# The first projection stage with on-chip transfers in place of the permutation matmul of the rotary embedding

## The chip, the cores and the metric

The kernel runs on one core of a Trainium2 chip. The metric is the device time of one execution in microseconds. Shown beside it is one execution taken by the hardware profiler. The engines are TensorE (PE; PEld is its weight load), VectorE (DVE), ScalarE (ACT), GpSimd (POOL) and SyncE (SP), which here only issues DMAs.

## The reference

The model has two blocks of the first kind (an attention mixer, then a gated linear attention mixer) and one block with pooling, convolution, forgetting attention and a mixture of experts. Only the first mixer's projection concerns us. For 1024 tokens and 256 context tokens it computes `h @ w_in` (1024 features in, 26 x 128 out), normalizes the q and k heads (64 features each), and rotates the q and k of the tokens, not those of the context:

```
def rope_1d(x, pos):
    m = x.shape[-1] // 2
    inv = ROPE_BASE ** (-jnp.arange(m, dtype=jnp.float32) / m)
    ang = pos.astype(jnp.float32)[:, None] * inv[None, :]
    cos = jnp.cos(ang)[:, None, :]
    sin = jnp.sin(ang)[:, None, :]
    x1 = x[..., :m].astype(jnp.float32)
    x2 = x[..., m:].astype(jnp.float32)
    return jnp.concatenate([x1 * cos - x2 * sin, x2 * cos + x1 * sin], axis=-1)
...
def rope_axial(x, rows, cols):
    h = x.shape[-1] // 2
    return jnp.concatenate([rope_1d(x[..., :h], rows), rope_1d(x[..., h:], cols)], axis=-1).astype(x.dtype)
...
def project(h):
    ...
    qa = rms_norm(qa.reshape(Bn, T, A_HEADS, HEAD_DIM), a_qn)
```

The halves of a rotated pair are 16 features each, so in blocks of 32 features the first 16 and the last 16 change places, with a minus sign on one of them.

## The kernel before

Features lie on the 128 partitions and tokens along the free axis. `gemm_phase` (line 375) runs a list of jobs. A 32-bit matmul such as `rot` or `headones` shows in the trace as two records. A job makes 128 output features for all 1280 tokens: 8 contraction steps, in each of them three products (high x high, high x low, low x high parts of 32-bit numbers), each over three tiles of 512, 512 and 256 tokens, into one of two PSUM accumulators. In the first projection stage there are 26 jobs. Jobs 0 and 2 to 13 are q or k ("rope"); job 1 and jobs 14 to 25 are stored as they are ("store"). Jobs 0 and 1 run interleaved.

The engines run their own programs and meet at semaphores:

- SP loads the weight tiles into a ring of three (line 527); tile w waits until the low half of tile w-3 has been made (w_lo).
- ScalarE rounds the weights (line 583) and, when a rope job's products are done, writes for each tile its square into `sq` (line 715) and the accumulator times the gain into `xg` (line 716). The latter gives `free`, the accumulator's release (acc_free in the order).
- TensorE computes the helper matmuls of a rope job inside the products of the next job: one tile after every second contraction step (line 1104, `rope_aux`). For a tile of tokens these are `rot` times `xg` (line 1077, the permutation) and `headones` times `sq` (line 1079, the sums of squares of each head). For the context tile only the second is made. Before the helper matmuls of tile r TensorE waits for `rope_done` of the tile before it.
- ScalarE makes the reciprocal root from the sums (lines 609 and 611). VectorE multiplies the permuted piece by the sine table (line 1001) and `xg` by the cosine table (line 1002), adds them (line 1003) and multiplies by the root in place (line 1006), which gives `rope_done`. Then the piece is split into high and low halves and stored.
- Later phases issue other transfers from SP that the rows below show: `wa` (two loads of 17 partitions x 512), `rank` (two of 16 partitions x 1280), `k_lo` and `q_stack` (64 partitions x 1280, twelve loads in a row), `q_rows` and `gate` (64 partitions x 2 x 128).
- VectorE and GpSimd also compute the conditioning vectors of the second block in this stage (line 569 loads, line 807 products). Three preparing steps of these stand behind jobs 2, 3 and 4 on VectorE; the second of them is a reciprocal over 2048 columns (line 794).

Of the kernel before, what the change touches and what calls it, by code (L numbers as in the profile page):

```python
# [19 lines left out]
ALU = mybir.AluOpType  # L20
# [3 lines left out]
P = 128  # L24
D = 1024
KD = D // P
T = 1024
CTX = 256
META = 16
L2 = META + T  # L30
X0 = META
# [37 lines left out]
def shape_constants():  # L69

    p = np.arange(P)
    parts = {}
# [3 lines left out]

    rot = np.zeros((P, P))
    for d in range(P):
        if d % 32 < 16:
            rot[d + 16, d] = -1.0  # L80
        else:
            rot[d - 16, d] = 1.0
    parts["rot"] = rot
    m = 16
# [3 lines left out]
    ang = np.zeros((P, T), np.float32)  # L88
    for d in range(P):
        pos = rows if d % HD < 32 else cols  # L90
        ang[d] = pos.astype(np.float32) * inv[d % 16]
    parts["cos"], parts["sin"] = np.cos(ang), np.sin(ang)

# [32 lines left out]

CONST_WIDTHS = [("ident", P), ("ones", P), ("headones", P), ("rot", P), ("causal", P), ("anti", P), ("invcnt", 2 * META)]
ROUTE_WIDTHS = [("before", P), ("tile_end", 7), ("tile_at", 16), ("spare_off", 16), ("tile_no", 15), ("bound", NTILE + 1), ("column", P),
# [246 lines left out]
def gemm_phase(nc, E, wts, jobs, feed, adaln=None, decay_rows=None, spill=None, restore=None, sums=False, branch=None):  # L375
# [7 lines left out]
    with ExitStack() as ctx:  # L383
# [54 lines left out]
        if "rope" in kinds:  # L438
            xg = sb("rope_x", [P, 1280])
            sq = sb("rope_sq", [P, 1280])  # L440
            tab = sb("rope_tab", [P, 2, T])
            t1 = sb("rope_t1", [P, 512])
            t2 = sb("rope_t2", [P, 512])
            rs = sb("rope_rs", [P, 512])
            slots = [t1[:], t2[:], sq[:, 0:512], sq[:, 512:1024]]
            aux = [ps("rope_ss", [P, 512]), ps("rope_rot", [P, 512])]
            tab_in, xg_ready, aux_done, rope_done, ms_ready, rs_ready = (
                sem(n) for n in ("tab_loaded", "xg_ready", "aux_done", "rope_done", "mean_square_ready", "rstd_ready"))
# [66 lines left out]
        def _(eng):  # L515
            def load_operand(i):
# [3 lines left out]
                eng.dma_start(staged(i), feed.src(k, off, n)).then_inc(fed_in[i % feed.ring], 16)  # L520

            if feed.src is not None:
                load_operand(0)
            for w in range(wts.loaded, NW):
                if w >= NSTG:
                    eng.wait_ge(w_lo, w - NSTG + 1)
# [8 lines left out]
                if w == 8 and spill is not None:  # L535
                    eng.dma_start(spill, E.X[:, :, 0:META + T]).then_inc(spilled, 16)
            if spill is not None:
                eng.wait_ge(spilled, 16)
# [218 lines left out]
        def _(eng):  # L757
# [220 lines left out]
            for i, j in enumerate(jobs):  # L978
# [7 lines left out]
                for t, (off, n) in enumerate(j.tiles):  # L986
# [9 lines left out]
                    elif j.kind == "rope":  # L996
# [3 lines left out]
                        if off < T:  # L1000
                            eng.tensor_tensor(t2[:, 0:n], aux[1][:, 0:n], tab[:, 1, off:off + n], ALU.mult)
                            chain(eng.tensor_tensor(t1[:, 0:n], xg[:, off:off + n], tab[:, 0, off:off + n], ALU.mult))
                            chain(eng.tensor_tensor(t1[:, 0:n], t1[:, 0:n], t2[:, 0:n], ALU.add))
# [61 lines left out]
        def _(eng):  # L1065
            pending = []

            def rope_aux(i, t):

                j = jobs[i]  # L1070
                off, n = j.tiles[t]
                r = ropes_tiles[i] + t
                eng.wait_ge(free[i % NA], free_before[i] + t + 1)
                if r >= 1:
                    eng.wait_ge(rope_done, r)
                if off < T:
                    eng.matmul(aux[1][:, 0:n], col(E.con, CONST_AT, "rot"), xg[:, off:off + n],
                               start=True, stop=True)
                eng.matmul(aux[0][:, 0:n], col(E.con, CONST_AT, "headones"), sq[:, off:off + n],
                           start=True, stop=True).then_inc(aux_done, 1)  # L1080
# [2319 lines left out]
```

## Time and profile before

| what | value |
|---|---|
| time, median of 3 runs | 3193.76 us (3188.72 to 3194.73) |
| profiled execution, span | 3193.8 us |
| TensorE busy | 2804.2 us (88%) |
| VectorE busy | 1667.6 us (52%) |
| ScalarE busy | 1295.7 us (41%) |
| first projection stage | about 57 to 498 us, its q/k part to about 345 us |

The profiled execution's span is its own time; it is that of the median run to the last digit shown. Busy time is a mean over stages with different limits, so a change in one stage is read in that stage alone: in which engine is never idle there, and in what it waits for when it is.

### The profile page before, as it was taken

The numbers are of one execution on the slowest core, as the hardware profiler recorded it, in microseconds if no ns is written. First come the engines' busy times: TensorE is split into PE (matmuls) and PEld (weight loads), VectorE is DVE, ScalarE is ACT, GpSimd is POOL, SyncE is SP. The second block draws the span as 40 slices with busy tenths as digits, with TensorE's granted clock in tenths as the row PEclk, the third lists the DMA queues.
The fourth block names the chain that finished last, engine by engine and source line by source line (L and its number), as shares of the span: only waits on it lengthen the run. The fifth ranks groups of instructions, "written<-read, shape, count | busy, mean of one in ns | idle before, by whom it ended". The sixth has DMA issues, their size and how long they took to land. (4 is left out here: it accounts for less than half of the span.)

```text
span 3193.8 us, 36080 instructions
## 1 busy us (share of the span) xinstructions
PE 2804.2 (88%) x13684; PEld 2195.4 (69%) x13684; DVE 1667.6 (52%) x2724; ACT 1295.7 (41%) x2204; POOL 191.9 (6%) x268
## 2 busy tenths in 40 slices
PE   7999998987887989995986999999989899588883
PEld 3777885656775868883664789987856588366772
DVE  5566544657775240013774355641135473588886
ACT  4444212446775141123442241111324411488886
POOL 0000000110000000000000000000000030011110
PEclk8999998999998999996888999999989999799997
DMA  5233444533303032222023222332263151489985
GB/s 230 97 132 119 167 148 126 150 96 106 76 25 114 14 140 89 89 73 94 32 84 120 79 94 91 127 106 92 104 174 81 34 190 53 168 310 346 325 297 210
DMA packets 143871, 415.33 MB, mean 130 GB/s; under 512 B 23586, under 2 KB 47906, under 8 KB 142420
## 3 DMA queue, kind: packets, MB, share of 16 engines
q1 hardware_dynamic: 101748, 272.91, 25.9%
q0 software_dynamic: 24208, 69.70, 6.6%
q10 hardware_dynamic: 17744, 70.43, 6.0%
q8 instruction: 109, 1.79, 0.2%
q14 instruction: 62, 0.51, 0.1%
HBM read 322.21 MB, written 106.47 MB: 134 GB/s over the span
## 5 line engine op out<-in xcount | busy, mean ns | idle before, releaser
L1100 PE MATMUL acc<-act_hi,w_hi 128*128 128x512 f32 (+3 forms) x2512 | 721.4, 376 | 61.2 <-DVE act_lo L857 40.7
L1100 PE MATMUL acc<-act_lo,w_hi 128*128 128x512 f32 (+3 forms) x2512 | 701.1, 368 | 0.0
L1100 PE MATMUL acc<-act_hi,w_lo 128*128 128x512 f32 (+3 forms) x2512 | 699.2, 367 | 0.0
L1100 PEld LDWEIGHTS acc<-act_hi,w_hi 128*128 128x128 f32 x2512 | 449.3, 189 | 164.3 <-DVE w_lo L762 55.7
L762 DVE TENSOR_TENSOR w_lo<-w_stage,w_hi 128x1024 fp32r<-128x1024 f32 x126 | 154.2, 1225 | 739.2 <-ACT w_hi L583 739.2
L1100 PEld LDWEIGHTS acc<-act_lo,w_hi 128*128 128x128 f32 x2512 | 447.0, 190 | 75.6
L1100 PEld LDWEIGHTS acc<-act_hi,w_lo 128*128 128x128 f32 x2512 | 446.0, 189 | 76.5
L583 ACT ACTIVATE w_hi<-w_stage 128x1024 fp32r<-128x1024 f32 x126 | 133.1, 1057 | 848.3 <-PE acc L1100 821.0
L2852 DVE SCALAR_TENSOR_TENSOR expert_lo<-expert_stage,params,expert_hi 128x512 fp32r<-128x512 f32 x248 | 172.1, 747 | 57.5 <-ACT expert_hi L2768 57.4
L1950 DVE TENSOR_REDUCE max<-scores 128x1 f32<-128x256 f32 (+6 forms) x256 | 117.2, 484 | 149.1 <-PE scores L2093 148.3
L2768 ACT ACTIVATE expert_hi<-expert_stage,params 128x512 fp32r<-128x512 f32 x248 | 162.9, 714 | 63.6 <-PE expert_out L3073 30.6
L2133 PE MATMUL outputs<-probs_t,v_ones 128*128 128x512 f32 (+2 forms) x392 | 172.1, 520 | 1.9 <-ACT probs_t L1894 1.9
L1894 ACT ACTIVATE probs_t<-scores_t 128x512 f32<-128x512 f32 (+4 forms) x196 | 100.3, 514 | 119.6 <-PE scores_t L2119 116.7
L2111 PE MATMUL scores_t<-q_stack,k_hi 128*128 128x512 f32 (+4 forms) x196 | 122.5, 625 | 2.5 <-ACT q_rows L1918 2.5
L1481 DVE TENSOR_REDUCE stats<-scores 128x1 f32<-128x1280 f32 (+1 forms) x72 | 100.7, 1398 | 44.1 <-PE scores L1593 44.1
L3062 PE MATMUL expert_up<-expert_hi,slots_hi 128*128 128x512 f32 x248 | 101.6, 409 | 7.1 <-DVE slots_lo L2860 7.1
L694 ACT ACTIVATE out_stage<-acc 128x512 f32<-128x512 f32 (+1 forms) x162 | 78.1, 545 | 64.7 <-PE acc L1100 64.7
L1408 ACT ACTIVATE probs<-scores,stats 128x1280 f32<-128x1280 f32 (+1 forms) x80 | 92.2, 1154 | 25.9 <-DVE stats L1482 24.8
L2089 PE MATMUL scores<-k_hi,q_stack 128*128 128x256 f32 (+6 forms) x256 | 95.1, 374 | 5.4 <-DVE max L1950 2.4
L3064 PE MATMUL expert_up<-expert_hi,slots_lo 128*128 128x512 f32 x248 | 98.4, 397 | 0.0
L3063 PE MATMUL expert_up<-expert_lo,slots_hi 128*128 128x512 f32 x248 | 98.0, 395 | 0.0
L2093 PE MATMUL scores<-k_lo,q_rows 128*128 128x256 f32 (+6 forms) x256 | 92.0, 366 | 0.0
(410 smaller groups left out, 4206.3 us busy)
## 6 DMA issues: line engine op xcount, KB each, us to landing
expert_stage<-in_exp_w SPq DMA_DIRECT2D x186, 512.0 KB, 5.8
w_stage<-in_w_in SPq DMA_DIRECT2D x43, 512.0 KB, 4.3
rope<-out_stage ACTq DMA_DIRECT2D x26, 640.0 KB, 3.6
proj<-out_stage ACTq DMA_DIRECT2D x26, 640.0 KB, 5.3
w_stage<-in_ab_w_in SPq DMA_DIRECT2D x26, 512.0 KB, 4.7
w_stage<-in_gla_w_in SPq DMA_DIRECT2D x25, 512.0 KB, 5.0
residual<-in_adaln_w POOLq DMA_DIRECT2D x24, 512.0 KB, 3.9
gates<-out_stage ACTq DMA_DIRECT2D x24, 512.0 KB, 3.3
```

The lines of the kernel that those rows point to most:

```text
L583: eng.activation(whi[:, w % 2, :], stage[:, w % NSTG, :], ACT.Copy).then_inc(w_hi, 1)
L762: eng.tensor_tensor(wlo[:, w % 2, :], stage[:, w % NSTG, :], whi[:, w % 2, :].bitcast(F32), ALU.subtract).then_inc(w_lo, 1)
L1100: mmi = eng.matmul(a[:, t, 0:n], lhs[:, j.w % 2, kb:kb + P], rhs[:, c0 + k, off:off + n], start=first, stop=last)
L1481: chain(eng.tensor_reduce(st[:, q % 4, 0, 0:u.rows], s, AX, ALU.max))
L1894: eng.activation(pT[0:w, q % 3, c0:512], ST[q % 2][0:w, c0:512], ACT.Exp, scale=SCALE).then_inc(exped, 1)
L1950: eng.tensor_reduce(mx[:, n % 2, h, pc:pc + 1], SP[p % 3][:, 0:k1 - k0], AX, ALU.max).then_inc(max_done, 1)
L2111: eng.matmul(s[:, c0:512], kh[:, c, tok:tok + P], qs[:, n % QS, c0:512], start=True, stop=False)
L2133: eng.matmul(O[n % 2][:, c0:512], v1[0:w, u.pair % VS, u.side, tok // P, :], pT[0:w, q % 3, c0:512], start=fox and b == 0, stop=b == len(u ...
L2768: ins = eng.activation(whi[:, n % R, c], stage[:, n % NS, c], ACT.Copy, scale=gain_of(2 * i + q))
L2852: ins = eng.scalar_tensor_tensor(wlo[:, n % R, c], stage[:, n % NS, c], gain_of(2 * i + q), whi[:, n % R, c].bitcast(F32), ALU.mult, ALU.s ...
L3062: eng.matmul(UP[j % 2][:], uh, wh, start=k == 0, stop=False)
L3064: mm = eng.matmul(UP[j % 2][:], ul, wh, start=False, stop=k == KD - 1)
```

## The change

The permutation matrix and its matmul go. The sine table carries the sign instead. For each rope job and each of its two token tiles, SP issues eight transfers from `xg` to the buffer that held the square sums (`E.sums`, no longer read in this stage). Each moves 16 partitions of 512 columns to the partitions 16 up or 16 down. They wait for `free` of this tile, and for `rope_done` of the same tile of the rope job before, since that was the last to read the buffer. In SP's program those of job i stand ahead of the load of weight tile i+5. VectorE makes the cosine product first, and then waits for all eight transfers of the tile before the sine product.

```diff
--- before.py
+++ after.py
@@ -74,13 +74,6 @@
     parts["ones"] = np.ones((P, P))
     parts["headones"] = (p[:, None] // HD == p[None, :] // HD)
 
-    rot = np.zeros((P, P))
-    for d in range(P):
-        if d % 32 < 16:
-            rot[d + 16, d] = -1.0
-        else:
-            rot[d - 16, d] = 1.0
-    parts["rot"] = rot
     m = 16
     inv = (np.float32(10000.0) ** (-np.arange(m, dtype=np.float32) / np.float32(m))).astype(np.float32)
     tok = np.arange(T)
@@ -89,7 +82,7 @@
     for d in range(P):
         pos = rows if d % HD < 32 else cols
         ang[d] = pos.astype(np.float32) * inv[d % 16]
-    parts["cos"], parts["sin"] = np.cos(ang), np.sin(ang)
+    parts["cos"], parts["sin"] = np.cos(ang), np.sin(ang) * np.where(p % 32 < 16, -1.0, 1.0)[:, None]
 
     s, c = p[:, None], p[None, :]
     parts["causal"] = s <= c
@@ -124,7 +117,7 @@
 
 
 
-CONST_WIDTHS = [("ident", P), ("ones", P), ("headones", P), ("rot", P), ("causal", P), ("anti", P), ("invcnt", 2 * META)]
+CONST_WIDTHS = [("ident", P), ("ones", P), ("headones", P), ("causal", P), ("anti", P), ("invcnt", 2 * META)]
 ROUTE_WIDTHS = [("before", P), ("tile_end", 7), ("tile_at", 16), ("spare_off", 16), ("tile_no", 15), ("bound", NTILE + 1), ("column", P),
                 ("token_hi", 2 * NTT), ("token_lo", 1), ("order", 4)]
 PARAM_WIDTHS = [
@@ -443,7 +436,9 @@
             t2 = sb("rope_t2", [P, 512])
             rs = sb("rope_rs", [P, 512])
             slots = [t1[:], t2[:], sq[:, 0:512], sq[:, 512:1024]]
-            aux = [ps("rope_ss", [P, 512]), ps("rope_rot", [P, 512])]
+            turned = E.sums[:, X0:X0 + T]
+            turned_in = [sem(f"turned_loaded{t}") for t in range(2)]
+            aux = [ps("rope_ss", [P, 512])]
             tab_in, xg_ready, aux_done, rope_done, ms_ready, rs_ready = (
                 sem(n) for n in ("tab_loaded", "xg_ready", "aux_done", "rope_done", "mean_square_ready", "rstd_ready"))
         ropes = [i for i, j in enumerate(jobs) if j.kind == "rope"]
@@ -519,9 +514,22 @@
                     eng.wait_ge(fed_lo, i - feed.ring + 1)
                 eng.dma_start(staged(i), feed.src(k, off, n)).then_inc(fed_in[i % feed.ring], 16)
 
+            def turn_pairs(i):
+
+                for t in range(2):
+                    eng.wait_ge(free[i % NA], free_before[i] + t + 1)
+                    if ropes_tiles[i]:
+                        eng.wait_ge(rope_done, ropes_tiles[i] - 2 + t)
+                    off, n = jobs[i].tiles[t]
+                    for r in range(0, P, 32):
+                        for to, of in ((r, r + 16), (r + 16, r)):
+                            eng.dma_start(E.sums[to:to + 16, X0 + off:X0 + off + n], xg[of:of + 16, off:off + n]).then_inc(turned_in[t], 16)
+
             if feed.src is not None:
                 load_operand(0)
             for w in range(wts.loaded, NW):
+                if w - 5 in ropes:
+                    turn_pairs(w - 5)
                 if w >= NSTG:
                     eng.wait_ge(w_lo, w - NSTG + 1)
                 eng.dma_start(stage[:, w % NSTG, :], wdram[w]).then_inc(w_in[w % NSTG], 16)
@@ -534,6 +542,9 @@
                     eng.dma_start(tab[:], E.tables).then_inc(tab_in, 16)
                 if w == 8 and spill is not None:
                     eng.dma_start(spill, E.X[:, :, 0:META + T]).then_inc(spilled, 16)
+            for i in ropes:
+                if i + 5 >= NW:
+                    turn_pairs(i)
             if spill is not None:
                 eng.wait_ge(spilled, 16)
 
@@ -998,8 +1009,9 @@
                         eng.wait_ge(aux_done, r + 1)
                         out = xg[:, off:off + n]
                         if off < T:
-                            eng.tensor_tensor(t2[:, 0:n], aux[1][:, 0:n], tab[:, 1, off:off + n], ALU.mult)
-                            chain(eng.tensor_tensor(t1[:, 0:n], xg[:, off:off + n], tab[:, 0, off:off + n], ALU.mult))
+                            eng.tensor_tensor(t1[:, 0:n], xg[:, off:off + n], tab[:, 0, off:off + n], ALU.mult)
+                            eng.wait_ge(turned_in[t], 128 * (ropes.index(i) + 1))
+                            chain(eng.tensor_tensor(t2[:, 0:n], turned[:, off:off + n], tab[:, 1, off:off + n], ALU.mult))
                             chain(eng.tensor_tensor(t1[:, 0:n], t1[:, 0:n], t2[:, 0:n], ALU.add))
                         eng.wait_ge(rs_ready, r + 1)
                         if off < T:
@@ -1073,9 +1085,6 @@
                 eng.wait_ge(free[i % NA], free_before[i] + t + 1)
                 if r >= 1:
                     eng.wait_ge(rope_done, r)
-                if off < T:
-                    eng.matmul(aux[1][:, 0:n], col(E.con, CONST_AT, "rot"), xg[:, off:off + n],
-                               start=True, stop=True)
                 eng.matmul(aux[0][:, 0:n], col(E.con, CONST_AT, "headones"), sq[:, off:off + n],
                            start=True, stop=True).then_inc(aux_done, 1)
```

On SP, at the start of the stage's weight loads, before: (w_stage is the ring of weights)

```order
10 L527 DMA w_stage<-in_ab_w_in 128x1024
11 L527 DMA w_stage<-in_ab_w_in 128x1024 [waits w_lo_ready_48] x23
12 L383 UNCONDITIONAL_BRANCH
13 L1801 UNCONDITIONAL_BRANCH [waits barrier_Pool_Activation_PE_DVE_SP_release]
14 L1818 DMA v_raw<-proj 128x1280
```

and in the changed kernel, where square_sums is the buffer that takes the permuted pieces:

```order
11 L535 DMA w_stage<-in_ab_w_in 128x1024 [waits w_lo_ready_48] x2
12 L526 DMA square_sums<-rope_x 16x512 [waits acc_free0_50]
13 L526 DMA square_sums<-rope_x 16x512 x7
14 L526 DMA square_sums<-rope_x 16x512 [waits acc_free0_50]
15 L526 DMA square_sums<-rope_x 16x512 x7
16 L535 DMA w_stage<-in_ab_w_in 128x1024 [waits w_lo_ready_48] x2
17 L526 DMA square_sums<-rope_x 16x512 [waits rope_done_76,acc_free0_50]
18 L526 DMA square_sums<-rope_x 16x512 x7
19 L526 DMA square_sums<-rope_x 16x512 [waits rope_done_76,acc_free0_50]
20 L526 DMA square_sums<-rope_x 16x512 x7
21 L535 DMA w_stage<-in_ab_w_in 128x1024 [waits w_lo_ready_48]
```

Between one weight load and the next there are now two groups of eight transfers, each group behind a wait for its tile.

On VectorE, the first rope job's two token tiles, before:

```order
71 L1001 TENSOR_TENSOR rope_t_68<-rope_rot,rope_tab 128x512 [waits aux_done_74]
72 L1002 TENSOR_TENSOR rope_t_67<-rope_x,rope_tab 128x512
73 L1003 TENSOR_TENSOR rope_t_67<-rope_t_67,rope_t_68 128x512 [waits dve_steps_52]
74 L1006 TENSOR_TENSOR rope_x<-rope_t_67,rope_rs 128x512 [waits rstd_ready_77,dve_steps_52]
75 L1001 TENSOR_TENSOR rope_t_68<-rope_rot,rope_tab 128x512 [waits aux_done_74]
```

and in the changed kernel:

```order
71 L1012 TENSOR_TENSOR rope_t_67<-rope_x,rope_tab 128x512 [waits aux_done_75]
72 L1014 TENSOR_TENSOR rope_t_68<-square_sums,rope_tab 128x512 [waits turned_loaded0_70]
73 L1015 TENSOR_TENSOR rope_t_67<-rope_t_67,rope_t_68 128x512 [waits dve_steps_52]
74 L1018 TENSOR_TENSOR rope_x<-rope_t_67,rope_rs 128x512 [waits rstd_ready_78,dve_steps_52]
75 L1012 TENSOR_TENSOR rope_t_67<-rope_x,rope_tab 128x512 [waits aux_done_75]
```

The two products have changed places, and the second of them waits for the transfers, one semaphore for each tile.

On TensorE, the helper matmuls of the first rope job's tile 1 among the products of the next job it meets, before:

```order
192 L1100 MATMUL acc_42<-act_hi,w_lo 128x512 x2
193 L1100 MATMUL acc_42<-act_hi,w_lo 128x256
194 L1077 MATMUL rope_rot<-rope_x,consts 128x512 [waits rope_done_75,acc_free0_50]
195 L1079 MATMUL rope_ss<-rope_sq,consts 128x512
196 L1100 MATMUL acc_42<-act_hi,w_hi 128x512 x2
197 L1100 MATMUL acc_42<-act_hi,w_hi 128x256
```

and in the changed kernel:

```order
191 L1109 MATMUL acc_42<-act_hi,w_lo 128x512 x2
192 L1109 MATMUL acc_42<-act_hi,w_lo 128x256
193 L1088 MATMUL rope_ss<-rope_sq,consts 128x512 [waits rope_done_76,acc_free0_50]
194 L1109 MATMUL acc_42<-act_hi,w_hi 128x512 x2
195 L1109 MATMUL acc_42<-act_hi,w_hi 128x256
```

One matmul instruction is gone; the waits that stood on it now stand on the sum of squares.

## Rows read from the trace of the kernel before

**Rows 1.** Busy time by stretch; columns: stretch, length, each engine, clock, DMA.

```profile
57.00:345.00 288.00, 275.47 (x1244) 211.98 (x1245) 180.25 (x260) 137.32 (x244) 7.11 (x13) 0.96 0.32 118
```

**Rows 2.** Longest wait of TensorE, 57 to 345 us: total, times, longest.

```profile
PE rope_rot L1077 <- DVE rope_x L1006: 7.2, 1, 7.2
```

**Rows 3.** Timeline of one q/k job: start, us, engine, line, operation, [idle before <-releaser].

```profile
213.19 0.75 PE L1100 MATMUL acc<-act_hi,w_hi 128*128 128x512 f32 x3
...
214.83 0.68 ACT L716 ACTIVATE rope_x<-acc,params 128x512 f32<-128x512 f32 x1
...
216.71 1.02 PE L1077 MATMUL rope_rot<-rope_x,consts 128*128 128x512 f32 x2
...
217.57 1.02 PE L1079 MATMUL rope_ss<-rope_sq,consts 128*128 128x512 f32 x2
...
218.63 0.69 DVE L1001 TENSOR_TENSOR rope_t<-rope_rot,rope_tab 128x512 f32<-128x512 f32 x1 [2.70 <-PE rope_ss L1079]
...
219.24 0.68 DVE L1002 TENSOR_TENSOR rope_t<-rope_x,rope_tab 128x512 f32<-128x512 f32 x1
...
220.68 0.69 DVE L1006 TENSOR_TENSOR rope_x<-rope_t,rope_rs 128x512 f32<-128x512 f32 x1
...
221.92 1.02 PE L1077 MATMUL rope_rot<-rope_x,consts 128*128 128x512 f32 x2
...
231.09 0.75 PE L1100 MATMUL acc<-act_hi,w_hi 128*128 128x512 f32 x3
```

**Rows 4.** Records of line 1077: ns min/median/max, first and last start, forms.

```profile
L1077 PE MATMUL rope_rot<-rope_x,consts x52: 590/594/1193, 95.1 to 329.8; 128*128 128x512 f32 x52
```

**Rows 5.** Timeline of SP's DMA issues, two places: start, time in the queue.

```profile
1454.50 0.31 SPq L2210 DMA_DIRECT2D wa<-in_wa_f  x1
1454.86 0.23 SPq L2211 DMA_DIRECT2D wa<-in_wa_b  x1
...
1456.36 0.42 SPq L2214 DMA_DIRECT2D rank<-proj  x1
1456.82 0.66 SPq L2218 DMA_DIRECT2D v_raw<-proj  x1
...
777.42 0.60 SPq L1311 DMA_DIRECT2D k_lo<-rope  x1
778.06 0.60 SPq L1311 DMA_DIRECT2D q_stack<-rope  x1
```

**Rows 6.** DMA issues by kind: count, KB each, median us to landing.

```profile
q_rows<-rope SPq DMA_DIRECT2D x40, 64.0 KB, 2.4
...
mixed<-o_t POOLq DMA_DIRECT2D x40, 64.0 KB, 2.0
...
router_w<-in_router_w SPq DMA_DIRECT2D x1, 80.0 KB, 1.8
```

**Rows 7.** Busy time around a job's start, columns as in rows 1.

```profile
213.00:217.00 4.00, 4.00 (x21) 3.32 (x21) 2.89 (x5) 3.61 (x7) 0.53 (x1) 1.00 0.88 337
...
220.00:230.00 10.00, 10.00 (x48) 7.76 (x47) 5.78 (x10) 3.68 (x7) 0.00 (x0) 1.00 0.00 0
```

**Rows 8.** Three pauses of TensorE, and the stretches right after them (as rows 1).

```profile
112.11 0.82 PE L1100 MATMUL acc<-act_hi,w_hi 128*128 128x512 f32 x3 [2.44 <-DVE w_lo L762]
...
2844.72 0.73 PE L3073 MATMUL expert_out<-expert_hi,hidden_hi 128*128 128x512 f32 x2 [2.19 <-DVE hidden_lo L2973]
...
2948.13 0.73 PE L3073 MATMUL expert_out<-expert_hi,hidden_hi 128*128 128x512 f32 x2 [1.85 <-DVE hidden_lo L2973]
...
113.00:116.00 3.00, 3.00 (x10) 2.42 (x10) 0.71 (x1) 3.00 (x4) 0.00 (x0) 0.50 0.77 259
...
2949.00:2953.00 4.00, 4.00 (x12) 3.14 (x11) 3.08 (x4) 1.61 (x3) 0.00 (x0) 0.57 0.96 370
2844.00:2850.00 6.00, 5.29 (x23) 4.40 (x24) 5.42 (x9) 4.62 (x8) 1.22 (x1) 1.00 1.01 376
```

**Rows 9.** VectorE at its reciprocal.

```profile
148.62 12.94 DVE L794 RECIPROCAL residual<-residual 128x2048 f32<-128x2048 f32 x1
```

## Prediction

> **What bounds the kernel now.** I read the split by stage first, then who TensorE waits for in this stage, then one job in order of time, then the records of single DMA issues. In the first projection stage TensorE is busy 275.5 of 288.0 us at a granted clock of 0.96 [rows 1]: it sets the pace. Its longest wait is 7.2 us, once, for VectorE's rotated piece [rows 2]. Every q or k job in the steady part looks like the one shown: it starts at 213.19 and the next at 231.09, a period of 17.90 us [rows 3]. I call the start S. Six groups of three matmuls take 3.52 us (213.19 to 216.71), then come the two helper matmuls of tile 0, and so on at every second contraction step. Inside the job one loop matters: the helper pair of tile 1 waits until tile 0 is rotated (rope_done). VectorE ended that at 220.68 + 0.69 = S+8.18, and TensorE wanted it at 221.92 = S+8.73 [rows 3]. The loop has only 0.55 us of slack.
>
> **What goes.** 26 permutation matmuls (13 q/k jobs, two tiles each), recorded as 52 pieces [rows 4]. From the start of the one to the start of the next helper matmul is 217.57 - 216.71 = 0.86 us, so 1.71 us a job with tile 1, and 13 x 1.71 = 22.2 us in all if nothing takes their place. VectorE's product with the sine table reads SBUF instead of PSUM: 0.69 against 0.68 us for the two kinds [rows 3], nothing. The consts load shrinks by 64 of 400 KB: 0.2 us at 337 GB/s [rows 7], beside other loads; I take 0.
>
> **What comes.** For each of 26 pieces SP issues eight transfers of 16 partitions x 512 (32 KB). They wait for acc_free, given when ScalarE has written the piece: 214.83 + 0.68 = S+2.32 [rows 3]; with a hop SP begins at S+2.40. VectorE needs all eight before its second product. The unknowns are the spacing of issues, s, and the time from issue to landing, L. The eighth lands at S + 2.40 + 7s + L.
>
> Spacing: two loads of 17 partitions x 512 started 0.36 us apart (1454.50, 1454.86), a load of 16 partitions x 1280 was followed by the next start after 0.46 (1456.36, 1456.82), and in a run of twelve loads of 64 partitions the starts lie 0.64 apart (777.42, 778.06) [rows 5]. The lower end is from pairs with little queued ahead, the upper from a long queue of larger ones. I take 0.46, the row with 16 partitions; the ends are 0.36 and 0.64. Landing: 1.8 us for an 80 KB load, 2.0 for a 64 KB store, 2.4 for a 64 KB load [rows 6]. I take 2.0, ends 1.8 and 2.4.
>
> So tile 0 lands at S + 2.40 + 3.22 + 2.0 = S+7.62. From the start of one product to the end of the last multiplication is 220.68 + 0.69 - 219.24 = 2.13 us [rows 3]; with hops rope_done comes at S+9.88. TensorE, without its permutation matmul, is there at S + 3.52 + 0.86 + 3.52 = S+7.90 (one helper matmul, six more groups). It pauses 2.0 us. Tile 1 next: its eight transfers are queued behind tile 0's, and land at S + 2.40 + 15 x 0.46 + 2.0 = S+11.3. VectorE comes to them after the helper matmul (217.57 to 218.63 is 1.06 us) and one product, S + 9.88 + 1.06 + 0.61 = S+11.55: just hidden. The chain from there is the old one and has its 0.55 us. Hence a job changes by 2.0 - 1.71 = +0.3 us.
>
> Not all 13 jobs are steady. Job 0's helper matmuls come late, inside job 2, so its transfers are hidden: -1.71. In the fourth q/k job VectorE is held by a reciprocal of 12.94 us [rows 9], which causes the 7.2 us wait: its transfers are long there when VectorE comes, the first permutation matmul was inside the wait, and only the second counts: -0.86. Eleven jobs stay: 11 x 0.3 = +3.2. Together +0.6 us.
>
> **The clock.** After a pause of 2.44 us the granted clock of 113 to 116 us was 0.50, the 1.2 GHz level. After 1.85 us at 2948 the next 4 us had 0.57. After 2.19 us at 2844 it stayed at 1.00 [rows 8]. A fall costs about 1.6 us (3 us at half is 1.5; 4 us at 0.57 is 1.7). New pauses of 2.0 us lie among these. I take a fall after 4 of 11, +6.4 us; ends 0 and all eleven, +17.6.
>
> **Behind the new waits.** On SP, the load of weight tile i+5 now stands behind the 16 transfers of job i. It issued at about S+2.8 and would at S+2.40 + 16 x 0.46 = S+9.8; its tile is rounded two jobs later, over 30 us away: 0. At 0.64 it would still be at S+12.6. On VectorE, behind the stopped product, stand the low halves, the conditioning products and the next weight split; their place follows the last helper matmul, which moves with TensorE: 0. The DMA engines are 0.88 busy in 213 to 217 (stores of the job before) and 0.00 in 220 to 230 [rows 7]. So only the first few transfers share them, and the eighth starts at S+5.6, when only the conditioning load is left; I add nothing, and up to 0.4 us is inside the upper L.
>
> The Trainium skill, "DMA: Bandwidth & Descriptors", section "Anatomy of one DMA — SWDGE (gpsimd) path", puts the fixed cost of a DMA at about 2.0 us; it adds that most of it is the receipt of the write, slowest at HBM. By that reason an SBUF target could land sooner than the store's row. No row here has one of both ends in SBUF, and each 0.1 us less would be 1.1 us less over the eleven jobs.
>
> **Sum.** +0.6 + 6.4 = +7.0 us on the profiled execution's 3193.8, which is also the median of the three runs (3193.76): 3200.8 us. Taken apart: -22.2 for the matmuls, +22.0 for eleven pauses, +0.9 for the matmul whose room the reciprocal's wait keeps, +6.4 of clock.
>
> **Rivals.**
> Short queue: s = 0.36, L = 1.8. Tile 0 lands at S+6.72, rope_done S+8.98, pause 1.1 us, no clock falls (1.1 us is below all pauses of rows 8). A job gains 0.6: 11 x -0.6 - 2.6 = -9.3, 3184.5 us. This is the other side of zero. For it: the two issues in rows 5 that are most like the new ones in size. Against it: they are only two, and a run of eight may fill the queue. It decides from a landing before S+7.3, where the pause is under 1.71.
>
> All hidden: the loop holds when tile 0 lands by S+5.6. With L = 2.0 that wants s of 0.17, half of the least row. Then all 21.4 us that are not absorbed by the reciprocal come out: 3172.4 us. The skill's same section gives about 50 ns for the sequencer's part of one DMA; 7 x 0.05 would land tile 0 at S+4.75 and give this same time. The trace does not agree as far as it goes: no issue of rows 5 is under 0.23 us, though none is a copy within SBUF.
>
> Long queue: s = 0.64, L = 2.4. Tile 0 lands at S+9.28, rope_done S+11.5, pause 3.6. Tile 1 lands at S+14.4, done at S+16.6, TensorE wants it at S + 11.5 + 0.86 + 3.52 = S+15.9: 0.7 more. A job loses 4.3 - 1.71 = 2.6, 11 x 2.6 - 2.6 = +26; with falls after most pauses (8 x 1.6 = 13) +39: 3233 us. For it: sixteen in a row is the longest run of issues in the stage, and the run in rows 5 holds 0.64. Against it: those move four times the partitions.
>
> That the change doesn't do what it says would show as a wait of VectorE on something other than the transfers; the transfers and waits are all in the program, so I give this no share of its own.
>
> **Chances.** Small loss (the forecast, 3191 to 3212): 0.43. Short queue: 0.23. All hidden: 0.10. Long queue and between (3212 to 3235): 0.24. What a measurement can tell from no change is about 0.2%, 6.4 us. The small loss lies half within it (0.22) and half above (0.21); the short queue 0.17 faster, 0.06 within. Faster 0.17 + 0.10 = 0.27, same 0.28, slower 0.21 + 0.24 = 0.45. The range for 8 in 10 leaves the ends of the outer cases: 3178 to 3226.
>
> **What would show it.** The 26 groups of permutation matmuls gone. SP's issues 0.4 to 0.5 us apart, the eighth landing 7.3 to 8 us after a job's start. TensorE's helper matmul of tile 1 waiting 11 times about 2 us for VectorE, VectorE's product waiting for the DMA, none for tile 1's. The 7.2 us wait still there. A clock at 0.50 for some 3 us after a few pauses. The weight loads later, nobody waiting for them. It is wrong if the pauses are under 1 us or over 3, if tile 1's transfers are waited for, or if the clock falls after every pause or none.

## The result and the profile after

The changed kernel takes 3231.35 us (median of 4 runs, 3229.51 to 3236.68) against 3194.24 us for the kernel before on the same chip: 1.0122 times as long, interval 1.0108 to 1.0135. The forecast was 3200.8 us, in a range that ended at 3226. The profiled execution grew by 35.0 us, to a span of 3228.8.

The page of the changed kernel shows TensorE with the same work in total as before, 2803.6 against 2804.2 us, although 26 matmuls have gone:

```profile
PE 2803.6 (87%) x13632; PEld 2196.1 (68%) x13632; DVE 1668.5 (52%) x2724; ACT 1294.9 (40%) x2204; POOL 193.0 (6%) x268
```

Something that makes matmuls longer has eaten the saving. The split by stage says what (stretch, length, then each engine, granted clock, DMA share, GB/s), first of the kernel after, then of the one before, each over its steady part:

```profile
57.00:380.00 323.00, 274.11 (x1181) 212.71 (x1182) 181.48 (x259) 137.09 (x243) 6.56 (x12) 0.90 0.38 124
95.00:380.00 285.00, 239.02 (x1021) 185.04 (x1020) 153.68 (x212) 117.27 (x210) 5.85 (x11) 0.90 0.41 131
```

```profile
95.00:345.00 250.00, 240.35 (x1084) 184.22 (x1083) 152.33 (x213) 117.40 (x210) 6.40 (x12) 0.97 0.34 123
```

The row of before has 9.7 us without TensorE, that of after 46.0, and the granted clock fell from 0.97 to 0.90. The waits of TensorE in 57 to 390 us, which answer to [rows 2] (total, times, longest):

```profile
PE rope_ss L1088 <- DVE rope_x L1018: 43.0, 12, 8.1
...
PE rope_ss L1088 <- ACT rope_x L727: 0.5, 1, 0.5
```

And those of VectorE, of which the wait for the transfers is one:

```profile
DVE rope_t L1014 <- DMA square_sums<-rope_x: 45.3, 17, 4.6
```

One job in order of time answers to [rows 3]. S is 204.93, the next S 227.22:

```profile
204.93 0.75 PE L1109 MATMUL acc<-act_hi,w_hi 128*128 128x512 f32 x3
...
207.27 10.10 SPq L526 DMA_DIRECT2D square_sums<-rope_x  x16
...
208.44 1.02 PE L1088 MATMUL rope_ss<-rope_sq,consts 128*128 128x512 f32 x2
...
213.68 0.69 DVE L1014 TENSOR_TENSOR rope_t<-square_sums,rope_tab 128x512 f32<-128x512 f32 x1 [3.49 <-DMA square_sums<-rope_x]
215.13 0.69 DVE L1018 TENSOR_TENSOR rope_x<-rope_t,rope_rs 128x512 f32<-128x512 f32 x1
215.97 2.04 PE L1088 MATMUL rope_ss<-rope_sq,consts 128*128 128x512 f32 x2 [2.99 <-DVE rope_x L1018]
217.03 2.05 PE L1109 MATMUL acc<-act_hi,w_hi 128*128 128x512 f32 x3
...
218.74 0.69 DVE L1014 TENSOR_TENSOR rope_t<-square_sums,rope_tab 128x512 f32<-128x512 f32 x1
...
223.26 0.60 PE L1088 MATMUL rope_ss<-rope_sq,consts 128*128 128x256 f32 x2
...
227.22 0.75 PE L1109 MATMUL acc<-act_hi,w_hi 128*128 128x512 f32 x3
```

Three things are to be seen. The issues begin at S+2.34 and the sixteen take 10.10 us, so s is about 0.63, and VectorE starts the second product of tile 0 at S+8.75. TensorE's helper matmuls of tile 1 then begin at 215.97 after a pause of 2.99 us. Their two pieces take 2.04 us and not 1.02: the clock is at its lower level. From them to tile 2's helper (223.26) pass 7.29 us, where before the like stretch was 4.35. Tile 1's own transfers are hidden in this job (the row at 218.74 has no wait). They are not in every job: of VectorE's 17 waits eleven are for tile 0 and six for tile 1, the longest of these at the end:

```profile
369.26 0.69 DVE L1014 TENSOR_TENSOR rope_t<-square_sums,rope_tab 128x512 f32<-128x512 f32 x1 [1.13 <-DMA square_sums<-rope_x]
```

None of the six shows as a wait of TensorE: its waits are eleven at tile 0's rotation, the one behind the reciprocal, and one of 0.5 us for ScalarE.

The clock around it, in stretches:

```profile
204.00:209.00 5.00, 5.00 (x27) 4.09 (x25) 3.63 (x6) 3.83 (x7) 0.53 (x1) 1.00 0.81 279
213.00:216.00 3.00, 0.03 (x1) 0.06 (x1) 2.07 (x3) 0.00 (x0) 0.00 (x0) 0.88 0.24 53
216.00:222.00 6.00, 6.00 (x14) 4.18 (x15) 3.36 (x5) 1.84 (x3) 0.00 (x0) 0.50 0.37 111
222.00:227.00 5.00, 5.00 (x27) 4.26 (x26) 2.05 (x4) 1.84 (x4) 0.00 (x0) 0.99 0.00 0
```

Six microseconds at 0.50 (1.2 GHz) follow the pause. So this job has a period of 22.29 us: 17.90 - 1.71 + 2.99 of pause + 2.94 of clock is 22.1; 0.2 us is left over.

**The ledger of the stage.** I added up (1 - clock) times the length over stretches of 1 us from 95 us on: 6.8 us lost before, 29.0 after. Pauses for the rotated piece: 7.2 before, 43.5 after. So +36.3 of pauses, +22.2 of clock, -22.2 of matmuls (the forecast's estimate; that the last two are equal is chance), together +36.3. The last helper matmul starts 37.0 us later than before (371.8 against 334.8):

```profile
L1088 PE MATMUL rope_ss<-rope_sq,consts x78: 377/591/1193, 95.0 to 371.8; 128*128 128x512 f32 x52, 128*128 128x256 f32 x26
```

The last helper matmul is 37.0 us later and the whole execution 35.0 us longer, so the change is inside the stage. The transfers' rows answer to [rows 5] and [rows 6]: the records of their issues (ns min/median/max), then the landing in 95 to 360 us:

```profile
L526 SPq DMA_DIRECT2D square_sums<-rope_x x208: 507/589/1406, 89.6 to 366.2; - x104
...
square_sums<-rope_x SPq DMA_DIRECT2D x190, 32.0 KB, 2.0
```

**When the clock falls.** In 1 us stretches the clock goes to 0.50 after every one of the eleven pauses. The net +22.2 has one more term: the kernel before lost 1.7 us after a pause of 2.44 us for w_lo, the first of [rows 8]. The changed kernel has the same pause, and the clock stays:

```profile
110.32 0.81 PE L1109 MATMUL acc<-act_hi,w_hi 128*128 128x512 f32 x3 [2.44 <-DVE w_lo L773]
...
110.00:114.00 4.00, 3.68 (x18) 2.95 (x18) 0.69 (x2) 3.57 (x5) 0.00 (x0) 1.00 0.90 271
```

So the falls after the eleven pauses cost 22.2 + 1.7 = 23.9 us, 2.2 each, and the length of a pause alone does not say whether the clock falls.

### The profile page after: what moved, and what is told of

Read it like the earlier page. It is cut to its first block and busy times, and to the rows that moved or that the text cites. A ratio compares the mean times of both kernels' runs of the same rounds, so it can differ in the third digit from the quotient of the medians.

```text
span 3228.8 us, 36209 instructions
## 1 busy us (share of the span) xinstructions
PE 2803.6 (87%) x13632; PEld 2196.1 (68%) x13632; DVE 1668.5 (52%) x2724; ACT 1294.9 (40%) x2204; POOL 193.0 (6%) x268
## 5 line engine op out<-in xcount | busy, mean ns | idle before, releaser
L1109 PE MATMUL acc<-act_hi,w_hi 128*128 128x512 f32 (+3 forms) x2512 | 732.1, 381 | 59.4 <-DVE act_lo L868 38.9
```

The source lines that it names most:

```text
L1109: mmi = eng.matmul(a[:, t, 0:n], lhs[:, j.w % 2, kb:kb + P], rhs[:, c0 + k, off:off + n], start=first, stop=last)
```

## The experiments

The theory to be tested was that SP's rate of issue sets the landing of the eighth transfer, and that the clock doubles the price. The rivals: the transfers disturb other traffic, or other traffic slows them (the stores of the job before and the conditioning load, 0.88 of the DMA engines in [rows 7]). Each edit is shown against the changed kernel, shortened where there are dots. The kernels with one transfer, with four of 16 partitions and with a quarter of the bytes leave part of the permutation out: they only time the stage and are no replacements. The start of the last helper matmul, 334.8 before and 371.8 after, shows what a version does in this stage alone.

**Transfers and matmuls together.** The permutation matmuls and VectorE's old order are back; the 208 transfers copy the cosine table into the unused buffer, and no product reads them. They wait for `free` and for the transfers that filled the buffer before, not for `rope_done`.

```diff
-eng.dma_start(E.sums[to:to + 16, ...], xg[of:of + 16, off:off + n])
+eng.dma_start(E.sums[to:to + 16, ...], tab[of:of + 16, 0, off:off + n])
...
+eng.tensor_tensor(t2[:, 0:n], aux[1][:, 0:n], tab[:, 1, off:off + n], ALU.mult)
...
+eng.matmul(aux[1][:, 0:n], col(E.con, CONST_AT, "rot"), xg[:, off:off + n], start=True, stop=True)
```

> The kernel before, with its permutation matmul, and beside it 208 transfers of the same size, number and time of issue on SP (their source is the cosine table, nobody waits for them but the reuse of their buffer). Theory 1 (the loss is the wait for the eight transfers of tile 0 and what it brings): the transfers by themselves cost nothing, job period 17.90 us as before, time 3194 within 3 us. Rival (traffic: 208 transfers disturb the weight loads, the stores and the conditioning loads that share the DMA engines): slower than before by 5 to 20 us, with longer waits for w_lo or for the stores.

Measured: 3195.02 us, ratio 1.0001 (0.9992 to 1.0010), last helper 334.7. The wait of 7.2 us is the only one of the kind, and the transfers land as fast as in the changed kernel. Its waits of TensorE for VectorE, and its landings in 95 to 345 us:

```profile
PE rope_rot L1096 <- DVE rope_x L1025: 7.2, 1, 7.2
...
square_sums<-rope_tab SPq DMA_DIRECT2D x201, 32.0 KB, 2.0
```

The traffic, the 208 issues and the later weight loads cost nothing by themselves that can be told from zero (the interval is 3 us to either side). The loss lies in waiting for the transfers.

**One transfer a tile, and four.** 

```diff
-for r in range(0, P, 32):
-    for to, of in ((r, r + 16), (r + 16, r)):
+for r in range(0, 32, 32):
+    for to, of in ((r, r + 16),):
-eng.wait_ge(turned_in[t], 128 * (ropes.index(i) + 1))
+eng.wait_ge(turned_in[t], 16 * (ropes.index(i) + 1))
```

With four, the outer loop stays as it was and the wait counts 64.

> The changed kernel with one transfer of 16 partitions a tile in place of eight; seven eighths of the permutation are left out. Theory 1: it lands at S+2.34+2.0 = S+4.3, before VectorE comes, TensorE has no new pause, all 21.4 us of matmuls come out: 3172 us, granted clock as before. Rival (a transfer's way through semaphores and a busy queue is late whatever the number): pauses of over 1 us stay, time above 3185.

> The changed kernel with four of the eight transfers of a tile (those upward left out). Theory 1 with 0.625 us an issue and 2.0 us to landing: tile 0 lands at S+2.34+3x0.625+2.0 = S+6.2, TensorE goes on at S+8.55 instead of S+7.9, a pause of 0.65 us, too short for the clock to fall: 11 x (0.65-1.71) - 2.6 = -14 us, 3180 us. Rival (clock falls after any pause): 3195 us.

Measured with one: 3189.92 us, 0.9977 (0.9968 to 0.9987), last helper 325.0. With four: 3200.10 us, 1.0020 (1.0009 to 1.0030), last helper 337.9. Fewer issues bring most of the loss back, as the theory says, but both were forecast too fast: four at 3180 us, one at 3172. A job of the kernel with one transfer (S = 207.23), and above it the records of all its issues:

```profile
L526 SPq DMA_DIRECT2D square_sums<-rope_x x26: 507/507/638, 89.8 to 314.5; - x26
...
206.45 0.81 ACTq L604 DMA_DIRECT2D rope<-out_stage  x2
...
209.13 0.53 POOL L580 DMA_DIRECT2D residual<-in_adaln_g  x1 [16.96 <-DVE mod_product L818]
...
209.58 1.57 SPq L526 DMA_DIRECT2D square_sums<-rope_x  x2
...
214.11 0.69 DVE L1014 TENSOR_TENSOR rope_t<-square_sums,rope_tab 128x512 f32<-128x512 f32 x1 [1.61 <-DMA square_sums<-rope_x]
...
216.40 1.10 PE L1088 MATMUL rope_ss<-rope_sq,consts 128*128 128x512 f32 x2 [1.11 <-DVE rope_x L1018]
```

A single transfer of 32 KB was used 4.53 us after its issue, with the two 640 KB stores of the job before issued 3.1 us and a 512 KB load issued 0.45 us before it. So there are two floors: the issues, and what is already on the DMA engines.

**A quarter of the bytes.** Eight transfers, 128 columns each.

```diff
-eng.dma_start(E.sums[to:to + 16, X0 + off:X0 + off + n], xg[of:of + 16, off:off + n])
+eng.dma_start(E.sums[to:to + 16, X0 + off:X0 + off + n // 4], xg[of:of + 16, off:off + n // 4])
```

> The changed kernel with all eight transfers, each of a quarter of the columns (16 partitions x 128, 8 KB); the other columns are not permuted. Theory 1 (a fixed price for each issue, whatever its bytes): issues still 0.6 us apart, pauses 3 us, 3231 us as the changed kernel. Rival (the bytes or the DMA engines' share set the spacing and landing): spacing falls toward 0.2 us, pauses under 1 us, 3175 to 3185 us.

Measured: 3224.67 us, 1.0084 (1.0069 to 1.0099), last helper 363.6. The issues are as long as before, and the landing of one is 1.8 us:

```profile
L526 SPq DMA_DIRECT2D square_sums<-rope_x x208: 507/589/1668, 89.5 to 358.6; - x104
...
square_sums<-rope_x SPq DMA_DIRECT2D x200, 8.0 KB, 1.8
```

An issue costs the same whether it moves 8 or 32 KB. A quarter of the bytes brought back 8.2 of the 37.0 us, half of the issues (and so half of the bytes) 33.9 (337.9, above). Of the 8.2 most is clock: in the same sum as in the ledger it loses 22.2 us in place of 29.0, because two early pauses, of 2.98 and 2.65 us, left the clock at 1.00.

**Filling the pause.** Three matmuls that nobody reads stand ahead of tile 1's helper, in all q/k jobs but the first.

```diff
+if t == 1 and i != ropes[0]:
+    for _ in range(3):
+        eng.matmul(aux[1][:], col(E.con, CONST_AT, "headones"), sq[:, 0:512], start=True, stop=True)
```

> The changed kernel with three spare 32-bit matmuls (0.86 us each, result unused) on TensorE just ahead of the helper matmul of tile 1, in every q/k job but the first: TensorE works through 2.6 of the 3.0 us in which it waits for VectorE. No data come sooner. Theory 1 (part of the loss is the granted clock falling to 0.50 after the pauses, 22 of the 37 us): the clock stays at 1.00 but for the wait at the reciprocal, the stage is shorter by about 20 us, 3208 to 3212 us. Rival (the clock's share is only what overlaps the waits): 3230 us, the same.

Measured: 3221.35 us, 1.0077 (1.0055 to 1.0100), last helper 361.5. The clock did what was expected: the lost clock from 95 us on is back at 6.8 us.

```profile
95.00:370.00 275.00, 253.08 (x1094) 186.35 (x1093) 154.09 (x212) 117.22 (x210) 5.85 (x11) 0.98 0.42 136
```

But only 10.3 of the 22.2 us came back, and the 3208 to 3212 us expected were missed. Two rows of a job show why:

```profile
214.20 1.10 PE L1091 MATMUL rope_ss<-rope_sq,consts 128*128 128x512 f32 x2 [0.41 <-DVE rope_x L1018]
219.25 0.67 PE L1091 MATMUL rope_ss<-rope_sq,consts 128*128 128x256 f32 x2 [0.46 <-DVE rope_x L1018]
```

At full clock TensorE comes sooner to tile 2, and waits there for tile 1 (22 waits instead of 12, 19.5 us). The slow clock had covered tile 1's transfers. The loop ahead of tile 1 stays as long as it was, and in most jobs 0.3 to 0.4 us of pause is left even with the filling (in four 0.8 to 3.0). So the clock was no separate item: part of what it cost had been cover for tile 1.

**Two queues.** Four transfers of each tile from SP (h = 0), four from GpSimd (h = 1).

```diff
+to, of = (r, r + 16) if h else (r + 16, r)
+eng.dma_start(E.sums[to:to + 16, ...], xg[of:of + 16, ...]).then_inc(turned_in[2 * h + t], 16)
```

> The changed kernel with four of each tile's eight transfers issued by SP and four by GpSimd at the same time. Theory by issue spacing alone: the last issue of tile 0 is at S+4.2 and lands at S+6.2, TensorE pauses 0.65 us, 3180 us. Theory with a floor (as the kernels with one and with four transfers showed: none of them was there before S+6.5 to S+7.3, since the DMA engines carry the stores of the job before and a conditioning load): pause 1.3 to 2 us as with four transfers, 3195 to 3202 us. Rival (one shared descriptor generator sets the spacing, two queues do not help): 3230 us.

Measured: 3222.92 us, 1.0090 (1.0071 to 1.0110), last helper 362.5. Halving the issues of each queue brought the last helper only 9.3 us forward, and all three expectations (3180, 3195 to 3202, 3230) were missed. Now the landing is late. In 95 to 360 us:

```profile
square_sums<-rope_x SPq DMA_DIRECT2D x96, 32.0 KB, 3.9
square_sums<-rope_x POOLq DMA_DIRECT2D x96, 32.0 KB, 4.0
```

The second floor takes over: what was issued earlier landed no earlier. The same run has a control. GpSimd's conditioning loads begin at 173.84; in the job of 131.48, ahead of them but with the stores of the job before in place, VectorE had the piece 3.92 us after the first issue, in place of 6.42 later on:

```profile
131.48 4.93 SPq L518 DMA_DIRECT2D square_sums<-rope_x  x8
131.74 3.82 POOL L518 DMA_DIRECT2D square_sums<-rope_x  x8 [13.18 <-ACT rope_x L731]
...
135.40 0.69 DVE L1019 TENSOR_TENSOR rope_t<-square_sums,rope_tab 128x512 f32<-128x512 f32 x1 [1.00 <-DMA square_sums<-rope_x]
```

**Pairs 32 apart.** The columns of the weights, the gains and the tables are laid out in another order, so that a pair lies 32 partitions apart; four transfers of 32 partitions do the work of eight.

```diff
-for r in range(0, P, 32):
-    for to, of in ((r, r + 16), (r + 16, r)):
+for r in range(0, P, 64):
+    for to, of in ((r, r + 32), (r + 32, r)):
```

> The changed kernel with the features of each q and k head laid out so that the rotated pairs are 32 partitions apart: four transfers of 32 partitions a tile instead of eight of 16, the same bytes. If the number of issues counts, as with four transfers of 16: pause 1.5 to 2 us, 3195 to 3202 us. If the bytes count: 3225 to 3232 us.

Measured: 3213.45 us, 1.0052 (1.0032 to 1.0072), last helper 354.1. Better than eight, worse than four of half the size, and outside both expected ranges: the landing is 2.7 us for 64 KB in place of 2.3. Its pauses of 2.1 to 4.0 us still brought the clock down.

**The traffic moved away.** One transfer, and the conditioning load held until tile 0 is rotated; or one transfer, and the stores of the job before held to about S+10.

```diff
+if f + 4 in ropes:
+    eng.wait_ge(rope_done, ropes_tiles[f + 4] + [o for o, _ in jobs[f + 4].tiles].index(0) + 1)
...
-store(i - 1)
+held.append(i - 1)
...
+if t == 1 and held:
+    store(held.pop())
```

The first two lines stand on GpSimd ahead of the conditioning load, the others on ScalarE.

> The kernel with one transfer a tile (seven eighths of the permutation left out), and with GpSimd's 512 KB conditioning load of each q/k job held back until tile 0 is rotated. With one transfer alone VectorE waited until S+6.9 (4.5 us after the issue) and TensorE paused 0.8 to 1.5 us. If the conditioning load makes it late: landing by S+5, no pause, about 10 us less than with one transfer (3180 us). If the stores of the job before make it late: no change (3190 us).

> The kernel with one transfer a tile (seven eighths of the permutation left out), and with ScalarE's two 640 KB stores of a q/k job issued one job later, at about S+10, instead of just before the next job starts. If the stores make the single transfer late (they fill the DMA engines from S to S+3.4): landing by S+5, no pause, about 3180 us. If the conditioning load does: no change (3190 us).

Measured with late loads: 3177.61 us, 0.9948 (0.9930 to 0.9966), last helper 313.8, landing 1.9 us. With late stores: 3180.61 us, 0.9955 (0.9941 to 0.9970), last helper 320.7, landing 3.1 us. With one transfer alone TensorE paused nine times for tile 0, 8.8 us together. Late loads leave one such pause (1.0 us), late stores seven (4.6 us together). The second floor is this traffic, the load more than the stores.

**Both moved, with all eight transfers, from one queue and from two.**

> The changed kernel, all eight transfers a tile from SP, with both the stores and the conditioning loads moved behind tile 0's rotation. Theory (the eighth transfer is late by its place in the queue, 0.63 us an issue, and lands 2.0 us after issue with or without traffic): pauses of 2.9 us remain, 3225 to 3231 us. Rival (traffic): pauses fall to 1 to 2 us, 3195 to 3205 us.

> The kernel that issues four transfers a tile from SP and four from GpSimd, with the stores and the conditioning loads moved behind tile 0's rotation. On two queues alone the transfers landed 3.8 us after issue at S+8.5 and the pause stayed 3 us. Theory (two floors, one of issue spacing and one of traffic, at nearly the same place; here both are gone): landing at about S+6.2, pause 0.7 us, 3180 to 3185 us. Rival (sixteen transfers in flight hold each other up, or GpSimd's issues are late): pause 2 to 3 us, above 3205 us.

One queue: 3238.32 us, 1.0135 (1.0118 to 1.0152), last helper 375.9; no gain at all, and above both expected ranges. Two queues: 3189.42 us, 0.9981 (0.9968 to 0.9994), last helper 324.5. From one queue, in one job (S = 201.74):

```profile
204.09 9.99 SPq L526 DMA_DIRECT2D square_sums<-rope_x  x16
...
212.69 2.04 PE L1097 MATMUL rope_ss<-rope_sq,consts 128*128 128x512 f32 x2 [2.90 <-DVE rope_x L1027]
213.11 0.53 POOL L582 DMA_DIRECT2D residual<-in_adaln_g  x1 [29.69 <-DVE rope_x L1027]
...
217.32 0.69 DVE L1023 TENSOR_TENSOR rope_t<-square_sums,rope_tab 128x512 f32<-128x512 f32 x1 [1.85 <-DMA square_sums<-rope_x]
```

and from two (S = 209.12):

```profile
211.47 4.93 SPq L518 DMA_DIRECT2D square_sums<-rope_x  x8
211.74 3.83 POOL L518 DMA_DIRECT2D square_sums<-rope_x  x8 [10.03 <-ACT rope_x L740]
...
215.50 0.70 DVE L1028 TENSOR_TENSOR rope_t<-square_sums,rope_tab 128x512 f32<-128x512 f32 x1 [1.11 <-DMA square_sums<-rope_x]
...
217.79 1.10 PE L1102 MATMUL rope_ss<-rope_sq,consts 128*128 128x512 f32 x2 [0.61 <-DVE rope_x L1032]
```

With one queue the pause stays at 2.90 us: in this job it is set by the issues, and by nothing on the DMA engines. The held load (213.11) now meets tile 1's transfers, which are waited for (1.85 us), so this version got worse; its expectation had left that out. With two queues and free DMA engines both floors are gone and the pause is 0.61 us. Neither edit does it alone: two queues alone brought the last helper 9.3 us forward, late traffic alone put it 4.1 us back, both together brought it 47.3 us forward (324.5). The median of 3189.42 us is still above the 3180 to 3185 expected. Whether the late loads alone would have been enough with two queues was not run.

**The context tile first.** On top of the pairs 32 apart, a rope job's tiles run in the order context, tile 0, tile 1, so a whole helper interval lies before the first rotated tile is wanted.

```diff
...
+[TILES1[2], *TILES1[:2]] if n >= 2 and kind[f][0] == "rope" else TILES1
...
```

> The kernel with pairs 32 apart (four transfers a tile), and with the context tile, which needs no transfers, first in each q/k job but the first. TensorE then asks for tile 0 at S+11.9 instead of S+7.9 and tile 0's transfers land at about S+8. Theory 1: no pause is left but the one at the reciprocal, 3172 to 3176 us, the granted clock as before, faster than both kernels by 0.5%. Rival (the tail of the job, tile 1 now last, makes ScalarE's rounding and the next job's pieces late): pauses of 1 us or more return at the first helper matmul, over 3185 us.

Measured: 3177.52 us, 0.9950 (0.9935 to 0.9965), last helper 315.9. The only waits of TensorE for a piece or its release are these:

```profile
PE rope_ss L1091 <- DVE rope_x L1023: 7.7, 1, 7.7
...
PE rope_ss L1091 <- DVE rope_x L1021: 1.7, 1, 1.7
PE rope_ss L1091 <- ACT rope_x L730: 1.0, 1, 1.0
```

This version computes the whole of it and beats both kernels, the one before by 0.5%. The transfers are the same as in the kernel above with its twelve waits; only the time between asking for the piece and needing it is longer. The 7.7 us stand behind the reciprocal, as before. The new order was not run on the kernel before, where that one wait is all that it could save.

**The runs in one table.** x is the time from the first issue of tile 0's transfers to the second product, p the pause of TensorE in the same job, for one steady job of each.

| version | x, us | p, us | last helper, us |
|---|---|---|---|
| eight, one queue (the change) | 6.41 | 2.99 | 371.8 |
| eight, one queue, traffic late | 6.31 | 2.90 | 375.9 |
| eight of 8 KB | 6.17 | 2.75 | 363.6 |
| eight, two queues | 6.42 | 3.01 | 362.5 |
| four of 64 KB | 5.84 | 2.42 | 354.1 |
| four of 32 KB | 5.04 | 1.61 | 337.9 |
| one | 4.53 | 1.11 | 325.0 |
| eight, two queues, traffic late | 4.03 | 0.61 | 324.5 |
| one, stores late | 4.02 | 0.61 | 320.7 |

In every row p is x - 3.42, within 0.01. Nothing else enters the pause of a steady job. For eight on one queue x is 7 times 0.63 + 2.0 = 6.4, for two queues 3 times 0.63 + 2.1 = 4.0 once the DMA engines are free. The rows between, with fewer issues and the traffic in place, do not follow that sum: four would give 3.9.

## Why the prediction was wrong

**The step that failed is the spacing of issues.** "I take 0.46, the row with 16 partitions": measured 0.63, so 7 x 0.17 = 1.2 us more for tile 0. TensorE came 0.15 us later than assumed (S+8.05, not S+7.90), and 2.0 + 1.2 - 0.15 is the measured 2.99 within 0.1. The row that held was the upper end, 0.64 in [rows 5]. Neither partitions (16 or 32) nor bytes (8 to 64 KB) change the spacing. A long run of issues is only part of the reason: with one transfer a tile the record was still 0.51 us, where the pair of loads in [rows 5] has 0.31 and 0.23, and in the run of sixteen that begins at 185.17 the next starts are 185.72 and 186.36, so the full spacing is there from the third on. What else lengthens it, such as both ends lying in SBUF, no run separates. The eleven pauses were forecast at 22.0 us. They measure 43.0 - 8.06 = 34.9, on average 3.2, since three are longer: 3.96, 4.15 and 3.63 (there a single issue took 1.33 us).

**"I add nothing" for the shared DMA engines** was right for the eighth transfer and would have been wrong for an early one: with seven issues ahead it starts after the worst is over, and the run with late traffic and one queue has the same pause. One job is an exception: at 185.17, just after two conditioning loads, the piece was there 7.57 us after the first issue and the pause was 4.15 us; with the traffic late that job had 6.57 and 3.15. Where transfers go out sooner, the stores and the conditioning load cost them up to 2.5 us (4.53 against 2.0). I had the row for it [rows 7] and read it right, but for this version alone.

**The clock.** I took a fall after 4 of 11 pauses at 1.6 us: 6.4. Measured 22.2, so this term is off by 15.8 us, more than the pauses (12.9). All of the eleven pauses were followed by the lower level, at 2.2 us each. The number of falls followed from the pause of 2.0: that lies among [rows 8], a pause of 2.99 lies above them. The run with four transfers, whose pauses are near the 2.0 of the forecast, bears this out: its later ones of 1.50 to 1.99 us kept the clock, those of 2.26 and 3.27 did not, and it lost 8.5 us where the kernel before lost 6.8. Over all runs no pause for a rotated piece of up to 1.99 us was followed by the lower level, and every one of 2.99 or more was. Between them it went both ways: with pairs 32 apart all from 2.07 to 2.86 us brought it, with a quarter of the bytes 2.98 and 2.65 did not.

**What held.** The landing of 2.0 us. The start of the issues at S+2.40 (2.34). Tile 1 hidden from TensorE, though not from VectorE, which waited for it in six jobs, and in part by the slow clock, as the filled pause showed. The reciprocal's wait takes the matmul's room: 8.06 against 7.2 us, +0.86 as worked out. Matmuls gone: -22.2. Weight loads later, nobody waiting. Of the prediction's own signs of being wrong all three came up: pauses over 3 us on average, waits for tile 1's transfers, a fall after every pause. The mechanism was right and the sizes were not, and the outcome was that of the rival with the long queue, 3233 us against 3231.35 measured. But that rival reached it with two errors that cancel: its landing of 2.4 (measured 2.0) and a further pause at tile 1 (none) made 47 us of pauses, 12 too many, and its 8 falls at 1.6 made 13 us of clock, 9 too few. I had held against it that the row of 0.64 moves four times the partitions, which was no reason.

**The rival "all hidden".** The row first: no issue of the 208 took less than 507 ns. The Trainium skill, "DMA: Bandwidth & Descriptors", section "Anatomy of one DMA — SWDGE (gpsimd) path", has some 50 ns for the sequencer's part of a DMA that GpSimd issues. The prediction carried it over to SP, which the section does not do; but GpSimd's own records in the run with two queues are 0.48 us. The trace agrees on neither queue, and the measurement decides. On queues, two together helped little while the DMA engines were busy (362.5 against 371.8), and much once they were free (324.5, against 375.9 from one). The same page of the Trainium skill, section "Rules for kernel authors", says that spreading over engines saves only the sequencer's issue time and no bandwidth; the runs agree, and here the issue time was 4.4 of 6.4 us (7 x 0.63).

**Open.** The version with the context tile first ends its q/k part 18.9 us earlier than before and the one with late loads 21.0, and their ratios are worth 16 to 17 us. Both intervals (11 to 21 and 11 to 22 us) hold the full gain, so nothing shows that any of it is given back. Why some pauses of 2.90 us brought no fall (3 with one queue and late traffic), and the same 2.44 us did in one kernel and not in the other, stays open. So does what sets the 0.63 us.

## What to carry to other kernels

Before a matmul is traded for transfers, count the issues between the piece and its use: here n issues on SP's queue cost (n - 1) times 0.63 us plus 1.8 to 2.0 of landing for 8 to 32 KB, and more when large transfers are under way. Take the spacing from rows of the same kind of transfer; where there are none, price the longest one. The sum has to fit in the slack of the loop. Where it doesn't, ask for the piece one interval sooner (here, by the order of the tiles) or use more partitions a transfer, before adding queues. When a pause is forecast near the longest that left the clock alone, price both sides: here the clock added 2.2 us to a pause of 3.2.

## What the runs showed of the hardware

- An issue of these transfers on SP's queue takes 0.51 us alone (one transfer a tile) and 0.59 as one of many, starts 0.63 apart, for 8, 32 and 64 KB alike. On GpSimd's queue the records are 0.48 us (the eight of the job above end in 3.83 us).
- A transfer within SBUF lands 2.0 us after its issue for 32 KB and 1.8 for 8 KB; behind a 512 KB load and two 640 KB stores VectorE had a single 32 KB transfer only after 4.5.
- 208 transfers of 32 KB that nobody waits for cost no measurable time (1.0001), and the stage's weight loads land in 3.8 us in that run (4.7 before).
- The lower clock after a pause of 2.99 us lasted 6 us (216 to 222) and cost 2.94; over the eleven pauses it cost 2.2 us each.
- The same pause of 2.44 us was followed by a clock of 0.50 in the kernel before (113 to 116) and of 1.00 in the changed one (110 to 114).
